# Issue order of the weight transfers of the fixed experts in a mixture-of-experts stage

## What is computed

```python
def hier_moe(x, router_g, router_g_b, router_e, router_e_b, w_gate, w_up, w_down):
    ...
    h = jax.nn.silu(jnp.einsum('btd,edf->btef', x, w_gate)) * jnp.einsum('btd,edf->btef', x, w_up)
    h = h * comb.astype(x.dtype)[..., None]      # comb is zero for the experts a token did not take
    return jnp.einsum('btef,efd->btd', h, w_down)
```

## Time and profile before

| what | value |
|---|---|
| median of 3 runs | 1995.43 us (1992.7 to 1995.72) |
| the profiled execution, its own time | 1995.09 us |
| its span (first to last instruction) | 1993.3 us |
| TensorE busy | 1783.9 us, 89% of the span |
| TensorE waiting for in_exp_w_up, both layers | 33.1 us in 6 waits |
| DMA queue q1 (hardware), q0 (software) | 202.22 MB, 116.84 MB |

### The profile page before, as it was taken

One profiled execution on the slowest core, in us unless ns is written; L12 is line 12 of the kernel. 1 busy time (PEld: TensorE's weight loads), 2 busy tenths in 40 slices (PEclk: granted clock), 3 DMA queues, 4 the chain that ended last, 5 costly groups with the idle time before them and its releaser, 6 DMA issues. The chain is left out here.

```text
span 1993.3 us, 23990 instructions
## 1 busy us (share of the span) xinstructions
PE 1783.9 (89%) x9376; PEld 1205.5 (60%) x9376; DVE 801.8 (40%) x1611; ACT 445.0 (22%) x949; POOL 374.9 (19%) x398
## 2 busy tenths in 40 slices
PE   8999888999999998989399888989999999889890
PEld 6877656788887453333178776658888865433330
DVE  4665355533333341111529553554333325411116
ACT  0125434211111121111410343441111111211111
POOL 0013045000000012254000230530000004123535
PEclk8997899999999989989689969999999999799895
DMA  9112036322232667895650130443222344788964
GB/s 286 35 56 87 27 98 195 91 84 85 80 101 75 246 262 317 333 380 195 232 145 1 56 113 1 150 143 117 85 85 77 106 146 178 289 324 350 395 266 179
DMA packets 141460, 322.40 MB, mean 162 GB/s; under 512 B 34862, under 2 KB 97060, under 8 KB 122852
## 3 DMA queue, kind: packets, MB, share of 16 engines
q1 hardware_dynamic: 102646, 202.22, 28.5%
q0 software_dynamic: 37200, 116.84, 16.9%
q10 hardware_dynamic: 1502, 1.80, 0.3%
HBM read 360.20 MB, written 29.48 MB: 195 GB/s over the span
## 5 line engine op out<-in xcount | busy, mean ns | idle before, releaser
L1722 PE MATMUL ps<-space,xT 128*64 128x512 f32 x864 | 241.3, 632 | 33.4 <-DMA space<-in_exp_w_up 33.1
L1240 PE MATMUL ps<-space 128*128 128x272 f32 x1024 | 250.3, 392 | 0.0
L444 PE MATMUL ps<-xT,space 128*128 128x272 f32 (+1 forms) x960 | 225.7, 399 | 0.8 <-DMA space<-in_w_in 0.8
L1240 PEld LDWEIGHTS ps<-space 128*128 128x128 f32 x1024 | 194.6, 190 | 40.1
L444 PEld LDWEIGHTS ps<-xT,space 128*128 128x128 f32 (+1 forms) x960 | 184.1, 192 | 42.0 <-DMA space<-in_w_in 1.1
L1248 PE MATMUL ps<-space 128*128 128x272 f32 x640 | 157.1, 392 | 0.0
L1722 PEld LDWEIGHTS ps<-space,xT 128*64 128x64 f32 x864 | 75.4, 145 | 133.6 <-issue 132.2
L1979 DVE SCALAR_TENSOR_TENSOR space<-space,ps 128x256 f32<-128x256 f32 x32 | 21.5, 670 | 316.6 <-ACT space L1820 316.6
L1248 PEld LDWEIGHTS ps<-space 128*128 128x128 f32 x640 | 121.6, 190 | 25.1
L1240 PE MATMUL ps<-xT,space 128*128 128x272 f32 x512 | 127.8, 392 | 0.0
L1635 PE MATMUL ps<-space 128*128 128x512 f32 x256 | 114.3, 607 | 6.1 <-PEq L244 6.1
(11 more groups left out here) (382 smaller groups left out, 2495.3 us busy)
## 6 DMA issues: line engine op xcount, KB each, us to landing
space<-in_w_in SPq DMA_DIRECT2D x44, 1024.0 KB, 5.5
space<-in_exp_w_down SPq DMA_DIRECT2D x32, 1024.0 KB, 14.4
space<-in_exp_w_gate SPq DMA_DIRECT2D x30, 1024.0 KB, 13.3
space<-in_exp_w_up SPq DMA_DIRECT2D x30, 1024.0 KB, 16.1
space<-in_w_o SPq DMA_DIRECT2D x8, 1024.0 KB, 6.0
space<-x_rows SPq DMA_DIRECT2D x16, 512.0 KB, 6.1
space<-y_rows SPq DMA_DIRECT2D x16, 512.0 KB, 6.6
x_rows<-space POOLq DMA_DIRECT2D x12, 512.0 KB
```

Of the source, the lines that this page charges most:

```text
L444: t = nc.tensor.matmul(ps[0:m, 2 * (n % 4) + h, 0:HN], w[:, f, c * P:c * P + m], k.xT[:, f, h, :], start=(f == 0), stop=(f == KD - 1))
L1240: t = m.matmul(out, w[:, f, :], x[:, f, :], start=(first and f == 0), stop=(f == H - 1), skip_group_check=True)
L1722: i = m.matmul(ps[r, 6 + t % 2, :], k.xgT[:, t % 2, f, r], gate_up_of(g)[:, f], start=(f == 0), stop=(f == KD - 1), skip_group_check=True)
```

## The change

The transfers of the fixed experts from place 3 on are issued from a list that is sorted by when the room comes free. The key of a gate and up pair is 2 x place, that of a down matrix 2 x place + 3, where place is that of the group whose room is taken: this is the order in which TensorE ends gate_up(p), gate_up(p+1), down(p). Each transfer keeps its wait.

```diff
+FETCHES = sorted((2 * place(earlier(e)) + 3 * part, e, part) for e in USES[len(ROUND):] if e < NE for part in range(2))
...
-            for e in USES[len(ROUND):]:
-                if e < NE:
+            for _, e, part in FETCHES:
+                if part == 0:
                     sp.wait_ge(*due(k, k.m_gu, place(earlier(e)) + 1))
                     gate_up(e)
+                else:
                     sp.wait_ge(*due(k, k.m_dn, place(earlier(e)) + 1))
                     down(e)
```

## The result

| | before | after |
|---|---|---|
| median of the runs | 1995.58 us (4 runs, 1992.7 to 1998.27) | 1949.16 us (4 runs, 1944.84 to 1950.56) |
| the profiled execution, its own time | 1995.09 us | 1950.56 us |

The ratio is 0.9767, with an interval of 0.9751 to 0.9782: the change is worth 2.3%. The forecast was 1959 us with a range from 1950 to 1971; the kernel came out 0.84 us under the range, at the time of the second rival, "all hidden". The gain is 46 us where 36 were forecast.

What follows compares the result with a forecast made beforehand. TensorE was taken to be held by late up matrices at places 4, 7 and 9 of both layers: 1995.09 - 45.5 + 9.3 given back at later gathers + 0.34 for the median gave 1959 us, range 1950 to 1971.

Steps and rivals of the forecast that it cites:

- all hidden: Rival outcome: nothing is given back at the later gathers, 1950 us; chance 0.12 for 1948 to 1953.
- The waits and their clock: Gate_ups at places 4, 7, 9 of both layers: up-matrix waits and slower matmuls behind them go, saving 45.5 us.
- What is delayed for it: Down matrices queued behind two gate and up pairs, 10 us more of queue: nothing waits, cost 0.
- Place 12: Its gather, slack 5.8 us, becomes 0.7 us late in layer 1 and 1.6 in layer 0.
- What is late next: Gathers behind place 9 asked for up to 22.3 us sooner in layer 1 become late; 9.3 us given back.
- place 15 of layer 1: Its gather, slack read as 0.4 us, becomes 6.1 us late, with 1.6 us more for clock.
- 15.8 us: Idle DMA time per layer from gate_up(1) to turn 12; transfers can come sooner only as much as it is filled.
- bound from below: Least given back at the later gathers: 0, if full engines work faster than in pieces; then 1950 us.
- Rival 1: Second half slower: both queues reach only 394 GB/s or other gathers wait; 1968, up to 1975 us; chance 0.25.
- Rival 3: A long-stretch DMA cap of 357 GB/s: waits only move, no idle time is filled, 1995 us; chance 0.04.
- Rival 4: Slower kernel because gathers of places 6 to 14 starve; 2022 us if each is 4 us late; chance 0.04.

Runs made afterwards that it cites:

- The last block by itself: Kernel before with only the pair of place 9 (experts 14, 15) in the new order; ratio 0.9919, stages 190.93 / 191.78 us.
- half the change: Kernel before with gates and ups ahead of downs inside places 3, 6 and 9 only, places 4 and 7 in old order; ratio 0.9854, stages 183.15 / 180.30 us.
- the second profile: The changed kernel run once more, unaltered, on another chip; ratio 0.9773 to the kernel before, stages 179.68 / 178.43 us.
- the cheap one: Kernel before with 3 MB more per layer copied right behind SP's last down, ahead of place 12's gather; ratio 1.0075, stages 204.31 / 204.00 us.
- the dear one: Kernel before with 3 MB more per layer issued after gate_up(11), ahead of place 15's gather; ratio 1.0075, stages 200.68 / 208.25 us.
- changed kernel with 3 MB: Changed kernel with 3 MB more per layer issued after gate_up(11), ahead of place 15's gather; ratio 0.9873, stages 181.28 / 187.89 us.

## Why the prediction was wrong in its size

**The waits and their clock: right.** It took off 45.5 us. The only loss named by a wait is 1.18 us at turn 12 of layer 0, and the stages are 44.6 us shorter. The last block by itself gave the 20.0 us of its own waits and clock. The cause, SP held by a down while room is free, is right too. The account of each wait by the late issue of its own matrix is not: with half the change the waits at places 4 and 7 went as well.

**What is delayed for it: right.** No down waits for its matrix (the last down of a layer waits 0.76 us for VectorE, as it did before with 0.75), the downs' median landing is 12.1 us, and no wait of a gate_up is left at a spare group.

**Place 12: right.** 0.7 and 1.6 us late were forecast; some 0.1 and 1.2 were measured. Loads and landings in both kernels confirm a slack of about 5 us before and none after, and the gather took 17.2 us to land after, where the prediction had 17.

**The failed step** is the one under "What is late next" on place 15 of layer 1: "Slack 0.4, so 22.3 - 0.4 - 15.8 = 6.1 us late", with 1.6 us of clock behind it. Turn 15 asked 22.7 us sooner (174.0 us behind gate_up(1) before, 151.3 after), and its gather was not late at all but had 1.5 us to spare. The step was 6.1 + 1.5 = 7.6 us off, from two terms (and 0.4 us the other way, 22.7 for 22.3).

- *The slack was about 5.4 us, not 0.4.* I took a burst of 354 small packets for the landing of this gather. Its own rows had all passed by 1910; the empty group behind it on the same queue makes the same kind of small packets. This is 5.0 us, the larger term. With it alone the prediction's sum gives 22.3 - 5.4 - 15.8 = 1.1 us late at place 15 and no clock lost there: 1995.09 - 45.5 + 1.6 + 1.1 + 0.34, about 1953.
- *The transfers came forward by more than 15.8 us.* The landing moved from 168.6 to 149.8 us behind gate_up(1), that is by some 18.7 us. This is 2.9 us.

Where the second comes from shows in the DMA view of the stretch from gate_up(1) to this landing, layer 1. Before (1741.43 to 1910.00), totals and the two queues with their share of the engines' time:

```profile
DMA packets 13412, 61.40 MB, mean 364 GB/s; under 512 B 5123, under 2 KB 5123, under 8 KB 6727
...
q0 software_dynamic: 9127, 30.18, 46.0%
q1 hardware_dynamic: 4278, 31.12, 45.3%
```

After, in the second profile, which has the landing (1700.98 to 1850.80):

```profile
DMA packets 13551, 62.16 MB, mean 415 GB/s; under 512 B 5170, under 2 KB 5170, under 8 KB 6774
...
q0 software_dynamic: 9263, 30.91, 51.4%
q1 hardware_dynamic: 4281, 31.14, 50.1%
```

The 61.40 MB of before would take 148.0 us at 415 GB/s in place of 168.6. Of these 20.6 us, 168.6 x (1 - 91.3 / 101.5) = 16.9 are idle engines, and 3.7 are rate while busy. Against them 0.76 MB more passed ahead of the landing, 1.8 us, which leaves 18.8. The shares are rounded, so this split is good to about half a us. The rate is there on both queues: q1 needed 0.453 x 168.6 / 31.12 = 2.45 us of full engines per MB before and 2.41 after, q0 2.57 and 2.49.

The prediction had the faster rate as its bound from below ("if the engines, kept full, do the work of these stretches faster than they did it in pieces") and gave it 0.12. Its two rows of 394 GB/s, 1837 to 1857 and 1874 to 1914, are not two readings of one limit, and it took the first for the pace of two busy queues. In the second only q0 had work, and the slow part is its first half. The windows of that stretch in two halves, before, and of the same work after (last two columns DMA share and GB/s):

```profile
1874.00:1894.00 20.00, 20.00 (x104) 7.85 (x102) 3.39 (x6) 3.84 (x6) 12.62 (x13) 1.00 0.98 368
1894.00:1914.00 20.00, 20.00 (x100) 7.28 (x98) 2.37 (x4) 2.49 (x5) 12.03 (x12) 1.00 1.02 421
```

```profile
1829.80:1849.80 20.00, 20.00 (x102) 7.74 (x100) 3.39 (x6) 3.71 (x6) 12.43 (x13) 1.00 1.02 412
1849.80:1869.80 20.00, 20.00 (x100) 7.32 (x98) 2.37 (x4) 2.52 (x5) 12.51 (x13) 1.00 1.02 419
```

(412 - 368) x 20 us = 0.88 MB, or 2.1 us, fell behind in those 20 us alone. Why they were slow is open: no run took it apart.

**The rivals.** Rival 2, all hidden, is what happened, at 1950. Its reason, the error of the landing times, is the larger part (5.0 us); what came forward beyond the 15.8 us is the smaller (2.9). Rival 1, a slower second half, is refuted by 416 GB/s behind turn 12. Rival 3 is refuted by 156 us at 414 to 416. Rival 4 needed each gather 2.5 us late on the average, and one was late, by 1.2. Its "q1 never runs dry" does not hold: behind the last down of SP only q0 has work.

**The range** ended at 1950 because that is where nothing is given back. It left nothing for the scatter of the runs, 1944.84 to 1950.56 for this kernel, and 1949.16 lies in that.

## What to carry to other kernels

When a queue waits for room in program order, sort its transfers by when the room comes free, and count the gain by the idle time of the DMA engines ahead of each wait, not by the delay of the one transfer that is waited for. Read the slack of what is late next from its landing, where the DMA view gives it, or from packets that can only be its own (here the 23 of 4 KB): a burst of small ones may belong to the transfer behind it. Check that with a load ahead of it, and read how far the landing itself moved, since 3 MB cost 7.7 us in one place and 10.0 in another. And when the engines go from interrupted to full, let the estimate of what they can carry run up to the best rate of the trace (here 409 GB/s over 33 us), not only down to the worst.

## What the runs showed of the hardware that I had not expected

**Empty rows cost turns, not bytes.** The DMA view of the kernel after, 1745 to 1751 us, while an empty spare group is on q0 and 1 MB matrices are on q1:

```profile
DMA packets 682, 2.51 MB, mean 418 GB/s; under 512 B 376, under 2 KB 376, under 8 KB 376
...
q1 hardware_dynamic: 341, 2.51, 99.9%
q0 software_dynamic: 341, 0.00, 3.3%
```

The two queues are served packet for packet, 341 each. The small ones take 3.3% of the engines' time, but each waits for a packet of the other queue, 2.51 MB / 341 = 7.4 KB on the mean, so q0 passes only 57 of its empty rows in a microsecond. q1 loses nothing. The Trainium skill (DMA: Bandwidth & Descriptors, Queues, rings and completion order) has the engines change queues at packet boundaries, with some 9 to 17 descriptors to a packet; the equal counts agree with the turns, and no run here shows how many descriptors one turn takes.

**A load of 3 MB does not always cost its bytes.** It moved a gather's landing by 7.7 us in one run and by 10.0 in another, both in the kernel before. The windows of stretches in which the loads were moved (last two columns DMA share and GB/s), the cheap one and then the dear one:

```profile
1820.00:1837.00 17.00, 15.43 (x64) 5.89 (x66) 1.69 (x3) 1.79 (x3) 4.67 (x5) 0.79 1.02 426
```

```profile
1863.90:1880.00 16.10, 16.10 (x83) 6.42 (x80) 3.32 (x6) 2.95 (x5) 10.96 (x11) 1.00 1.00 369
```

The engines were full in both stretches, at 426 and at 369 GB/s. The cause is open, as is that of the 368 GB/s above.

**Where a short wait starts to cost more than itself.** The gate_up behind a wait of 1.18 us took 7.09 us, and so it did behind 1.48 us (half the change, turn 12 of layer 1); behind 1.79 us it took 8.78 (changed kernel with 3 MB, turn 14 of layer 1). These are single cases.

**The same kernel differs from chip to chip by over half of what the change is worth.** The kernel before took 1965 us on one chip and 1996 on another, 1.6%, and from 1950 to 1975 on one chip alone, while the stages of the kernel after agreed to 0.02 us between two chips (179.67 and 179.68, 178.41 and 178.43). Their two profiled executions, 1950.56 and 1931.94 us, differ outside the stages: 13.1 us ahead of gate_up(1) of layer 0 (759.29 and 746.15) and 5.9 us between the stages. What differs there was not looked for.
